# Around an expert stage: earlier gathers, a later slot table, down weights ordered one pair later, and two tiles of a projection moved ahead of it

## The reference, cut to what matters

```python
x = x + mixed @ w_out                       # output projection
h = rms_norm(x, ln_moe)
group = softmax(h @ w_router_group + b)     # 8 groups, the best one
top-2 of the 8 experts of that group        # 64 experts in all
for each expert: y = (silu(h_e @ w_gate) * (h_e @ w_up)) @ w_down   # 1024 -> 256 -> 1024
x = x + sum over the two experts of gate * y
ple_gate = sigmoid(rms_norm(x, ln_ple) @ w_ple_gate)
x = x + ple_gate * (p @ w_ple_proj)         # p: 1024 x 256, w_ple_proj: 256 x 1024
return rms_norm(x, ln_final)
```

## Time and profile before

| | us |
|---|---|
| median of 3 runs | 1636.62 (1636.1 to 1639.54) |
| profiled execution, its own time | 1637.01 |
| its span in the profile | 1635.3 |
| PE busy | 1443.3 (88%) |
| DVE / ACT / POOL busy | 549.6 / 362.6 / 256.2 |
| moved by SP's queue | 289.16 MB |
| moved by POOL's queue | 16.80 MB |

### The profile page before, as it was taken

One profiled execution on the slowest core, in us unless ns is written; L12 is line 12 of the kernel. 1 busy time (PEld: TensorE's weight loads), 2 busy tenths in 40 slices (PEclk: granted clock), 3 DMA queues, 4 the chain that ended last, 5 costly groups with the idle time before them and its releaser, 6 DMA issues. The chain is left out here.

```text
span 1635.3 us, 17248 instructions
## 1 busy us (share of the span) xinstructions
PE 1443.3 (88%) x6050; PEld 770.9 (47%) x6050; DVE 549.6 (34%) x875; ACT 362.6 (22%) x663; POOL 256.2 (16%) x378
## 2 busy tenths in 40 slices
PE   6999999689989999999999577778788786889997
PEld 4456844344457777775555332323233232234443
DVE  3332033323126766664354421211111111114443
ACT  2222132100025555553221100001000010004222
POOL 1000000100014443343110011111111111110110
PEclk9999999889999999999999698989989898899999
DMA  5221045522441112104311479999999999992231
GB/s 185 77 65 65 0 154 147 152 69 84 108 137 39 39 39 67 42 6 190 119 52 59 178 302 417 394 397 409 397 401 398 399 406 399 404 387 83 77 113 41
DMA packets 107225, 306.49 MB, mean 187 GB/s; under 512 B 22304, under 2 KB 60848, under 8 KB 81328
## 3 DMA queue, kind: packets, MB, share of 16 engines
q1 hardware_dynamic: 97680, 289.16, 47.1%
q0 software_dynamic: 9504, 16.80, 2.7%
HBM read 283.85 MB, written 39.90 MB: 198 GB/s over the span
## 5 line engine op out<-in xcount | busy, mean ns | idle before, releaser
L1576 PE MATMUL pe_gu<-w_gu,xT 128*64 128x512 f32 x1024 | 273.1, 695 | 105.6 <-DMA w_gu<-in_w_expert_up 102.9
L251 PE MATMUL ps<-wide,gst 128*128 128x512 f32 x640 | 284.5, 605 | 3.1 <-DVE wide L404 3.1
L1576 PEld LDWEIGHTS pe_gu<-w_gu,xT 128*64 128x64 f32 x1024 | 83.7, 158 | 273.2 <-issue 271.3
L251 PEld LDWEIGHTS ps<-wide,gst 128*128 128x128 f32 x640 | 123.2, 194 | 153.9 <-issue 152.4
L1782 DVE TENSOR_TENSOR hs<-sg,pe_gu 128x256 f32<-128x256 f32 x32 | 13.5, 421 | 377.8 <-ACT sg L1692 377.8
L832 DVE TENSOR_TENSOR_SCAN Pm<-rem,Pm 128x128 f32<-128x128 f32 (+3 forms) x96 | 107.8, 1123 | 76.4 <-ACT brk L766 76.3
L1310 PE MATMUL p_x<-wide,pw 128*128 128x512 f32 x256 | 114.8, 602 | 2.1 <-DVE mx L1177 1.4
L1594 PE MATMUL pe_y<-wide,hTe 128*64 128x512 f32 x512 | 115.4, 592 | 1.1 <-DVE ys L1787 1.1
L928 POOL TENSOR_TENSOR wt<-brk,Pm 128x128 f32<-128x128 f32 (+3 forms) x96 | 88.5, 922 | 164.7 <-DVE Pm L832 162.6
L265 PE MATMUL psk<-w_tok,wide 128*128 128x260 f32 (+1 forms) x384 | 111.7, 453 | 0.0
L1665 PE MATMUL pe_y<-w_gu,xT 128*128 128x512 f32 x256 | 111.2, 592 | 0.0
(11 more groups left out here) (288 smaller groups left out, 1531.9 us busy)
## 6 DMA issues: line engine op xcount, KB each, us to landing
w_gu<-in_w_expert_gate SPq DMA_DIRECT2D x64, 1024.0 KB, 13.8
w_gu<-in_w_expert_up SPq DMA_DIRECT2D x64, 1024.0 KB, 15.9
wide<-in_w_expert_down SPq DMA_DIRECT2D x64, 1024.0 KB, 9.1
gst<-in_w_in SPq DMA_DIRECT2D x20, 512.0 KB, 4.3
wide_tab<-y_d SPq DMA_DIRECT2D x8, 1024.0 KB, 5.7
qkv_d<-y_sb SPq DMA_DIRECT2D x12, 512.0 KB, 2.6
qk_st<-rows_d SPq DMA_DIRECT2D x8, 768.0 KB, 7.2
gst<-qkv_d SPq DMA_DIRECT2D x8, 768.0 KB, 5.3
```

The lines of the kernel that those rows point to most:

```text
L251: last = pe.matmul(ps[s][:, c], w_ct[:, s, k, :], hT[:, k, c], start=k == 0, stop=k == KT - 1)
L1576: last = pe.matmul(p_gu[e * CAP:(e + 1) * CAP, :], xT[:, s, k, e * CAP:(e + 1) * CAP], wv[:, e, :, k, :], start=k == 0, stop=k == KT - 1)
```

## The change

Five edits.

1. **First gathers.** `token_at`, `token_ok` and `xg_in` live through both stages. The gathers of pairs 0 and 1 are issued by POOL at the end of `stage_output_projection`, once the rows of `h_d` are stored and `tab_ok` is set, instead of at the start of the pass. A later pass's first two gathers are issued at the end of the pass before it (so the last pass issues two gathers whose slots are all empty).
2. **Later table.** The 32 table matmuls of the next pass move from behind `hidden(0)` to ahead of `gate_up(31)`; DVE's comparison stays at pair 0 (`next_slots`), its conversion moves to pair 31 (`next_table`).
3. **Order of the weight loads.** SP issues `load_gate_up` for pair q+3 ahead of `load_down` for pair q+2.
4. **Two tiles of p's projection.** SP loads `w_ple_proj` and p ahead of the four down loads. PE transposes two tiles of p ahead of `route(7)` and runs three halves of their projection ahead of `earlier(7)`, the fourth at the stage's end; ACT copies them out (the copy of the transposes stands ahead of `h_copy(7)`). The embedding part keeps tiles 2 to 7.
5. **Routing's order.** `choose` is split into `choose_group` and `choose`; `place(5)` moves ahead of `add_to_x(7)`; the ranks of tile 5 are computed between the two halves of tile 7's projection; the ranks of tile 7 get another PSUM bank; `table(6)` goes behind the counts.

```diff
+EARLY = 2
 # output projection, SP
 sp.wait_ge(mm_done, NT)
+sp.dma_start(w_p, A["w_ple_proj"][0].rearrange("(p k) c -> p k c", k=PT)).then_inc(S["p_in"], 16)
+sp.wait_ge(x_ok, NT)
+sp.dma_start(p_all, A["p"][0, 0].rearrange("(t p) c -> p t c", p=P)).then_inc(S["p_in"], 16)
 for s in range(2):
     load_down(sp, A, S, s, s)
-sp.dma_start(S["w_p"], ...).then_inc(S["p_in"], 16)
-sp.wait_ge(x_ok, NT)
-sp.dma_start(S["p_all"], ...).then_inc(S["p_in"], 16)
 # POOL, at the stage's end
+for s in range(2):
+    pool.wait_ge(h_out[s], 16 * (NT // 2 + 1))
+pool.wait_ge(S["tab_ok"], 1)
+for s in range(2):
+    pool.tensor_copy(S["token_at"][:, s:s + 1], tab[:, 1, s:s + 1]).then_inc(S["token_ok"], 1)
+    pool.wait_ge(S["token_ok"], s + 1)
+    pool.indirect_dma_start(out=h_sb[:, s, :], ...).then_inc(S["xg_in"][s], 16)
 # ACT, at the stage's end
+act.wait_ge(ep_done, 1)
+act.activation(pT..., p_m[:, 0:EARLY * PT, :]..., ACT.Copy).then_inc(epT_ok, 1)
 h_copy(NT - 1)
+for t in range(EARLY):
+    for h in range(2):
+        copy_e(t, h)
 # DVE
 place(NT - 4)
+choose_group(NT - 3)
 choose(NT - 3)
+place(NT - 3)
 add_to_x(NT - 1, 1, NT // 2 - 1)
 biases(NT - 2)
+choose_group(NT - 2)
 norm_h(NT - 1, 1, NT // 2 - 1)
-place(NT - 3)
 choose(NT - 2)
-place(NT - 2)
 biases(NT - 1)
+choose_group(NT - 1)
 choose(NT - 1)
+place(NT - 2)
 place(NT - 1)
 # PE
 h_transposes(NT - 1, 1)
+pe.wait_ge(S["p_in"], 32)
+turn_p()
 route(NT - 1)
 earlier(NT - 2)
 within(NT - 2)
 table(NT - 3)
-table(NT - 2)
+embed(0, 0)
+embed(0, 1)
+embed(1, 0)
 earlier(NT - 1)
 within(NT - 1)
 ... counts ...
+table(NT - 2)
 table(NT - 1)
+embed(1, 1)
 # experts, SP
-with sp.Fori(0, NL) as j:
-    for s in range(2):
-        x = (b * (NP - 2) + j * 2 + (2 + s)) % NP
-        sp.wait_ge(gu_done, b * NP + j * 2 + (s + 2))
-        load_gate_up(sp, A, S, x, s)
-        sp.wait_ge(y_done, b * NP + j * 2 + (s + 2))
-        load_down(sp, A, S, x, s)
+gate_up_behind(0, 0)
+with sp.Fori(0, NL - 1) as j:
+    for r in range(2):
+        gate_up_behind(2 * j + (1 + r), 1 - r)
+        down_behind(2 * j + r, r)
+gate_up_behind(NP - 3, 1)
+down_behind(NP - 4, 0)
+down_behind(NP - 3, 1)
 # experts, POOL
-pool.wait_ge(tab_ok, b + 1)
-pool.wait_ge(xt_done, b * NP + 1)
-gather(column(0), 0, b * NP)
-gather(column(1), 1, b * NP + 1)
 ...
 scatter(column(NP - 1), 1, b * NP + (NP - 1), b * NPS + NL)
+pool.wait_ge(tab_ok, b + 2)
+pool.wait_ge(xt_done, b * NP + (NP + 1))
+for s in range(2):
+    gather(...)
 # experts, PE: first() loses and last() gains, ahead of gate_up(31)
 pe.wait_ge(hot_ok, b + 1)
 for i in range(2 * NT): ... p_tab matmuls ...
 # embedding
-turn_p(0)
-turn_p(1)
+turn_p(EARLY)
+turn_p(EARLY + 1)
 pe.wait_ge(ys_ok, n * NP + 1)
-for t in range(NT - 1):
+for t in range(EARLY, NT - 1):
     embed(t)
 # DVE: tiles 0 and 1 are read from e_first; norm(0), norm(1) also wait for xg_in
```

More of the change, by code:

```diff
@@ L1217, in first_of_max, with choose_group @@
                     link(dve.tensor_reduce(out, cand[:], AX.X, ALU.min))
[L1219 removed]
+                def choose_group(t):
                     at = slice(t, t + 1)
@@ L1305, in turn_s, with project @@
                     last.then_inc(str_done, 1)
[L1307 to L1312 removed]
+                def project(s, k0, h):
+                    for k in range(k0, k0 + HK):
+                        last = pe.matmul(p_x[:, h, :], mT[:, s, k, :], w_o[:, k, h * 512:h * 512 + 512],
+                                         start=k == 0, stop=k == KT - 1)
+                    if k0 and h:
                         last.then_inc(mm_done, 1)
@@ L1360, in step @@
                     pe.wait_ge(sT_ok, t + 1)
-                    project(s, HK)
+                    project(s, HK, 0)
+                    if last:
+                        earlier(t - 2)
+                        within(t - 2)
+                    project(s, HK, 1)
                     if not first:
                         route(t - 1)
-                    if t >= 2:
+                    if t >= 2 and not last:
                         if t == 2:
@@ L1373, in _, with turn_p, embed @@
                     step(t, t % 2, t // 2, t == 0, t == NT - 1)
+                def turn_p():
+                    for t in range(EARLY):
+                        for k in range(PT):
+                            last = pe.transpose(p_m[:, PT * t + k, :], p_all[:, t, k::PT], ident[:])
+                    last.then_inc(ep_done, 1)
+                def embed(t, h):
+                    pe.wait_ge(epT_ok, 1)
+                    if t == 0:
+                        pe.wait_ge(x_ok, NT)
+                    else:
+                        pe.wait_ge(ee_ok, 2 * t - 1 + h)
+                    for k in range(PT):
+                        last = pe.matmul(p_x[:, h, :], pT[:, t, k, :], half(w_p[:, k, :], h), start=k == 0, stop=k == PT - 1)
+                    last.then_inc(ee_done, 1)
                 for t in range(NT - 3):
@@ L1605, in first, with body, last @@
                         hidden(n0)
+                    def body(q, s, j, r):
+                        gate_up(s, n0 + q, b * NL + j + (1 + r))
+                        down(r, n0 + q - 1, b * NL + j + 1)
+                        tokens(r, n0 + q + 1, b * NPS + j + 1)
+                        hidden(n0 + q)
+                    def last():
                         pe.wait_ge(hot_ok, b + 1)
@@ L1922, in build_program @@
         S["y_out"] = [whole.enter_context(nc.semaphore(f"y_out{s}")) for s in range(2)]
-        for name in ("p_in", "tab_ok"):
+        S["xg_in"] = [whole.enter_context(nc.semaphore(f"xg_in{s}")) for s in range(2)]
+        for name in ("p_in", "tab_ok", "token_ok"):
             S[name] = whole.enter_context(nc.semaphore(name))
```

124 lines of the change are left out of this document (68 added, 56 removed).

## The result

The changed kernel takes **1614.61 us** (median of 4 runs, 1613.15 to 1614.91) against 1637.71 (4 runs) beside it: a ratio of 0.9859, 95% interval 0.9847 to 0.9871. Predicted were 1612.5, range 1605 to 1622. The profiled execution took 1614.38, its span is 1612.6 against 1635.3: 22.7 us shorter, where the prediction had 24.1.

The account below looks back on a forecast made before the run. The weight stream (DMA share 0.99 at 400 GB/s) was taken to bound the expert pass. Terms 4.4 - 10.6 - 5.0 - 5.2 + 1.0 - 1.4 - 7.3 = -24.1 us off the 1635.3 span gave 1611.2, forecast 1612.5 us, range 1605 to 1622.

Parts of the forecast that it names:

- The hole at 949: Expert pass, 949.2 to 959.8 us: the empty load queue gets filled once the table matmuls move and loads issue earlier, -10.6 us.
- small holes: Expert pass, 976 to 1438 us: short dips in DMA share, 6 us in all, mostly vanish with earlier weight loads, -5 us.
- order at the end: Pass's end: pair 30's down weights now stand behind pair 31's gate and up weights, so pair 31 starts earlier, -5.2 us.
- table at the end: Ahead of `gate_up(31)`: 32 table matmuls partly hidden in PE's wait of 4.41 us, +1.0 us, bounds 0 and +3.
- 1443 to 1446: Sign that the forecast is right: pair 31's `gate_up` stands at about this time in us, taking 7.1 us.
- the clock's -1.4: Pass's end: PE, kept busy, runs `gate_up(31)` at full clock, 8.50 to 7.1 us, -1.4 us, bound 0.
- Embedding: Embedding part after the experts: two tiles fewer of p's projection, 2 × 3.67 us, -7.3 us, bound -5.
- The margin: Embedding: ACT's scaling, started late behind `w_ple_gate`, catches up with PE's tiles with 0.5 us to spare.
- rival C: Every pair: PE waits for down weights now behind the next 4 MB; slower, about 1657 us; chance 0.03.
- rival B: Pass's end: pair 31's down weights or `w_ple_gate` bound it; 5.2 us and part of 7.3 lost, about 1620 us; chance 0.16.
- The start: Routing stage to first expert pair: `gate_up(0)` at 932.2 instead of 927.83 us, +4.4 us, bounds -0.2 and +8.7.
- p's landing: Routing stage: `w_ple_proj` lands at 900.7 us, then p's 1.05 MB, read at 264 GB/s, at 904.7 us.

Follow-up runs that it names:

- the experiment: The changed kernel with SP's old order of weight loads put back, all else unchanged: ratio 0.9954 to the kernel before.

## Why the prediction was right, point by point

- **The hole at 949 (-10.6), small holes (-5), order at the end (-5.2), table at the end (+1.0).** The sum is right to 0.1 us: -19.8, in part by luck; only `gate_up(31)` itself, at 1441.4, lies just ahead of the 1443 to 1446 that I had named, by the first stretch's 1.45 us among others. Undone singly, in that stretch, the table's place is worth 7.4 (predicted 9.6) and the order of the loads 10.6 (10.2): one term too large, and 1.7 us that appear only with both undone. The small holes are right (4.8 us gone, and 5.5 back with the old order). The order's own 5.2 had the right size and the wrong place: they were argued from the last pair and appear at the first reloads, as a hole of 5.2 us (share 0.14 from 960 to 966 us in the experiment). The order of the stream is changed once, at its head, and every pair after that is earlier by it. Before the change this delay and the table's lay one behind the other: pair 3's loads were issued 32.6 us behind `gate_up(0)`, against 25.8 with the old order alone, 28.5 with the old table alone and 19.9 now.
- **The table's +1.0 and the clock's -1.4.** `gate_up(31)` is at 7.09 us, and moving the table one pair earlier shows 0.8 us of net cost where the two terms together say a gain of 0.4, less than the scatter of the stretch.
- **Embedding (-7.3).** From `gate_up(31)` to `gate` 8.7 us less, predicted 8.7. The margin sufficed: ACT waits 1.89 us for `w_ple_gate`, and PE does not notice. How large it was is not measured.
- **Down weights (rival C), something behind the stream (rival B).** Not there: no wait of PE for down weights, in spite of a median landing of 19.6 us. The 1.5 us that the prediction left for `down(31)` were enough, since its load met a nearly empty queue.
- **The start (+4.4): the term that was mis-sized.** Measured +7.4. Every step of it up to the second gather instruction is within 0.8 us (`route(7)` starts 0.8 us sooner and takes 0.7 longer than predicted), and `tab_ok` and the gathers' end are within 0.5. The step that failed is "everybody waits for it at the block's end: about 927.1": the end waits not for the instruction but until its data have landed, 3 us more. The prediction had read the block's end from a block that held no gather. (Its 927.1 is also 0.4 us more than 922.3 and 4.4 add up to; the measured 4.7 us for that step make the slip good.)
- **p's landing.** I took 8.8 us from the first load, from the reading rate of 1 KB pieces, against 6.8 as an estimate by the Trainium skill's fit (DMA: Bandwidth & Descriptors, Anatomy of one DMA), which the page gives for a single DMA issued by GpSimd, while these two are issued by SP. Measured were 8.3, so the trace does not agree: by that fit p would have landed 1.5 us too early. How much of the 1.5 us is due to the 1 KB pieces no run shows; the second load was issued 1.25 us behind the first.
- **The first 1.45 us** were no part of the change, as the repeat of the changed kernel shows (897.2 for the same load), and stand at the program's start already. What makes its first 57 us vary is not known.

What four of the edits are worth, each undone alone, in the stretches that it touches: the order of the loads 10.6, the table's place 9.1, the early tiles 2.2, the early gathers -1.1, in all 20.8 of the 21.3 measured. (By the whole length they are 11.6, 9.3, 1.1 and -1.8, the last two below its scatter.) That p and `w_ple_proj` are loaded first, and edit 5, were not tried by themselves.

## What to carry to other kernels

When work is moved ahead of a barrier, price two things that it brings: the data still in flight at the barrier, and what stands behind it in program order on the same engine. Here two tiles worth 7.3 us at the end brought 1 to 2 us, and reordering the same instructions (what others wait for first, the movable work last) brought 5.5 more at the start. When two causes lie on one hole, ask what the hole would be if the other cause were gone: the hole of 10.6 us had the table and the wait for `down(0)` in it, and either alone leaves a hole of its own. And once a queue is full, ask for the landing of the last piece, not for the mean share.

## What the runs showed of the hardware

- A block's end waits for the data of indirect DMAs issued in it: the next block's first work came 0.5 us behind the last landed piece in three profiles, 3.4 to 3.5 us behind POOL's second gather instruction, 2.9 behind a single one. The wait runs beside other work of POOL's (0.9 us behind 3.7 us of iotas). Without a gather ACT went on 0.34 us after its own last work.
- PE's clock at a matmul group follows what PE did before: at the pass's end `gate_up` took 7.09 us (2.4 GHz) in each row above where PE had idled at most 1.6 us ahead of it, and 8.5 to 10.1 where it had idled 3.2 to 4.8 us. In the changed kernel's 10.10 us the granted clock is 0.50 (1.2 GHz) from 1423 to 1429. After 2.6 to 2.9 us of idling both were seen (7.09, and 8.78 in three kernels). `gate_up(0)`, which follows a long idle stretch, took 8.5 to 9.9 in every profile.
- With a full queue the pieces of a load do not land together: the last piece of a pair's 4 MB came 14 us behind the middle one after 30 pairs with a share of 1.00, and 5 us behind it where the queue had small holes. That one engine lags is my reading of single last pieces 2.5 us apart; the records do not name engines.
